# Reordering the routing stage: the shared expert's rows turned and copied earlier, one down product cut in two around the first expert's turned rows

## What is computed

```python
scores = sigmoid(x @ router_w)              # 512 x 64
# the best 4 of 8 groups of experts, in them the best 8 experts of a row
routed = for each expert e: (silu(xb @ w_gate[e]) * (xb @ w_up[e])) @ w_down[e], times the row's weight
shared = (silu(x @ sh_gate) * (x @ sh_up)) @ sh_down      # inner width 256
out = ALPHA * x + routed + shared
```

## Time and profile before

| what | value |
|---|---|
| median of 3 runs | 1092.02 us |
| the profiled execution's own time | 1090.4 us |
| its span, first to last instruction | 1088.6 us |
| PE busy | 1059.9 us, 97% |
| DVE, ACT, POOL busy | 853.4 (78%), 716.7 (66%), 237.1 us (22%) |
| mean granted TensorE clock | 0.997 |
| DMA moved | 294.80 MB, mean 271 GB/s |

### The profile page before, as it was taken

One profiled execution on the slowest core, in us unless ns is written; L12 is line 12 of the kernel. 1 busy time (PEld: TensorE's weight loads), 2 busy tenths in 40 slices (PEclk: granted clock), 3 DMA queues, 4 the chain that ended last, 5 costly groups with the idle time before them and its releaser, 6 DMA issues.

```text
span 1088.6 us, 15813 instructions
## 1 busy us (share of the span) xinstructions
PE 1059.9 (97%) x5382; PEld 864.9 (79%) x5382; DVE 853.4 (78%) x906; ACT 716.7 (66%) x819; POOL 237.1 (22%) x173
## 2 busy tenths in 40 slices
PE   5999999999999999999999999999999999999996
PEld 4778877778888767888888888888888888888585
DVE  6654345663355788999999999999999999999476
ACT  3431244451242527888889988888998888888643
POOL 1000000000005120333333333333333333332101
PEclk9999999999999999999999999999999999999998
DMA  8532221214356449999999999999999999999831
GB/s 296 196 117 78 78 78 39 79 39 155 116 199 237 155 133 347 366 388 391 384 379 384 392 372 392 395 389 388 382 385 374 392 385 390 382 390 342 271 120 61
DMA packets 72571, 294.80 MB, mean 271 GB/s; under 512 B 15312, under 2 KB 18384, under 8 KB 47696
## 3 DMA queue, kind: packets, MB, share of 16 engines
q1 hardware_dynamic: 52944, 256.43, 60.0%
q0 software_dynamic: 19008, 35.71, 12.7%
q10 hardware_dynamic: 576, 2.10, 0.5%
HBM read 283.67 MB, written 44.04 MB: 301 GB/s over the span
## 4 chain that ended last, share of the span: by engine, by line
PE 92%; DMA 3%; DVE 2%; ACT 1%; issue 1%; SPq 0%; DVEq 0%; POOLq 0%; ACTq 0%
PE ps L416 26%; PE ps L418 25%; PE ps L417 25%; PE ps L1562 5%; PE ps L1586 1%; PE ps L1275 1%; PE ps L753 1%; PE ps L777 1%; PE ps L764 1%; DMA residual_rows<-y,put_idx 1%; DMA raw<-in_w_in 1%; DVE w_lo L400 1%; PE ps L325 1%; ACT w_hi L395 1%; PE ps L1546 0%
## 5 line engine op out<-in xcount | busy, mean ns | idle before, releaser
L1825 DVE TENSOR_TENSOR w_lo<-gu_raw,w_hi 128x2048 fp32r<-128x2048 f32 x128 | 292.3, 2284 | 1.0 <-ACT w_hi L1673 1.0
L1673 ACT ACTIVATE w_hi<-gu_raw 128x2048 fp32r<-128x2048 f32 x128 | 245.0, 1916 | 0.0
L416 PE MATMUL ps<-w_hi,xgT_hi 128*128 128x512 f32 x512 | 200.1, 391 | 0.8 <-issue 0.8
L418 PE MATMUL ps<-w_hi,xgT_lo 128*128 128x512 f32 x512 | 199.8, 390 | 0.0
L417 PE MATMUL ps<-w_lo,xgT_hi 128*128 128x512 f32 x512 | 199.2, 389 | 0.0
L1830 DVE TENSOR_TENSOR dn_lo<-dn_raw,dn_hi 128x2048 fp32r<-128x2048 f32 x62 | 142.2, 2293 | 20.8 <-ACT dn_hi L1682 20.8
L416 PE MATMUL ps<-w_hi,act_hi 128*128 128x512 f32 x368 | 146.6, 398 | 0.0
L418 PE MATMUL ps<-w_hi,act_lo 128*128 128x512 f32 x368 | 143.7, 390 | 0.0
L417 PE MATMUL ps<-w_lo,act_hi 128*128 128x512 f32 x368 | 143.4, 390 | 0.0
L1682 ACT ACTIVATE dn_hi<-dn_raw 128x2048 fp32r<-128x2048 f32 x62 | 118.8, 1917 | 0.0
L416 PEld LDWEIGHTS ps<-w_hi,xgT_hi 128*128 128x128 f32 x512 | 96.1, 188 | 21.3 <-issue 1.3
(11 more groups left out here) (218 smaller groups left out, 1763.6 us busy)
## 6 DMA issues: line engine op xcount, KB each, us to landing
gu_raw<-in_moe_w_gate SPq DMA_DIRECT2D x64, 1024.0 KB
gu_raw<-in_moe_w_up SPq DMA_DIRECT2D x64, 1024.0 KB
dn_raw<-in_moe_w_down SPq DMA_DIRECT2D x62, 1024.0 KB
raw<-in_w_in SPq DMA_DIRECT2D x18, 1024.0 KB, 5.2
h_rows<-x_rows SPq DMA_DIRECT2D x8, 512.0 KB, 4.5
raw<-in_w_out SPq DMA_DIRECT2D x4, 1024.0 KB, 4.9
ple_raw<-in_ple_w_gate SPq DMA_DIRECT2D x4, 1024.0 KB, 9.9
x_rows<-in_x SPq DMA_DIRECT2D x4, 512.0 KB, 10.0
```

The lines of the kernel that those rows point to most:

```text
L416: nc.tensor.matmul(out, x_hi, w_hi, start=first, stop=False)
L418: return nc.tensor.matmul(out, x_lo, w_hi, start=False, stop=last)
L1673: nc.scalar.activation(m.w_hi[:, 2 * x.b + half], m.gu_raw[:, 2 * x.b + half], ACT.Copy).then_inc(gu_hi, 1)
L1825: nc.vector.tensor_tensor(m.w_lo[:, 2 * x.b + half], m.gu_raw[:, 2 * x.b + half], m.w_hi[:, 2 * x.b + half].bitcast(F32), ALU.subtract).th ...
```

## The change

On PE, `turn_h(0)` and `turn_h(1)` move up, between the halves of `gate_up(3)`; `turn_h(2)` goes ahead of `down(0)` and `turn_h(3)` behind it; `down(1)` is cut into its two halves, with `turn_x(0)` and the weights' locating between them; the wait for all four copies ahead of `turn_x(0)` becomes one for three, with the fourth ahead of `rounds`; `locate(3)` moves out of the routing into step 0, between the halves of `gate_up(0)`. On ACT, the copies of the turned tiles 0 and 1 go ahead of `silu(3)`, and that of tile 2 ahead of the high parts of expert 1's weights. On DVE, the work between `weigh` and the second `add_rows` is put in another order. No computation is added or removed.

```diff
-    def down(self, pe, t):
+    def down(self, pe, t, halves=(0, 1)):
...
-        for c in range(2):
+        for c in halves:
...
-        last.then_inc(self.summed, 1)
+        if halves[-1] == 1:
+            last.then_inc(self.summed, 1)
...
                 gate_up(x, 0)
+                if first and at == 0:
+                    locate(x.next(3))
...
         routing.gate_up(pe, 3, 0, 4)
         routing.count(pe)
+        routing.turn_h(pe, 0)
+        routing.turn_h(pe, 1)
         routing.gate_up(pe, 3, 4, KD)
         pe.wait_ge(routing.index_base, 1)
         for q in range(2):
             pe.wait_ge(hot_ready, q + 1)
             locate_part(Expert(0, 0, q), ROW_COLS + 8 * q, 0, rows_located)
-        routing.turn_h(pe, 0)
-        routing.turn_h(pe, 1)
+        routing.turn_h(pe, 2)
         routing.down(pe, 0)
-        routing.turn_h(pe, 2)
         routing.turn_h(pe, 3)
-        pe.wait_ge(routing.hT_ready, NT)
+        routing.down(pe, 1, halves=(0,))
+        pe.wait_ge(routing.hT_ready, NT - 1)
         turn_x(Expert(0, 0, 0))
         pe.wait_ge(routing.weighed, 1)
         for q in range(2):
             locate_part(Expert(0, 0, q), WEIGHT_COLS + 8 * q, 3, located)
-        routing.down(pe, 1)
+        routing.down(pe, 1, halves=(1,))
         locate(Expert(0, 0, 2))
-        locate(Expert(0, 0, 3))
+        pe.wait_ge(routing.hT_ready, NT)
         rounds(pe, body, embedding.tensor)
...
         routing.silu(act, 2)
-        routing.silu(act, 3)
         routing.copy_hT(act, 0)
         routing.copy_hT(act, 1)
+        routing.silu(act, 3)
+        routing.copy_hT(act, 2)
         split(Expert(0, 0, 1), 0)
         split(Expert(0, 0, 1), 1)
-        routing.copy_hT(act, 2)
         routing.copy_hT(act, 3)
...
         routing.weigh(dve)
+        one_hot(Expert(0, 0, 2))
+        find_weights()
+        split_x(Expert(0, 0, 0))
+        one_hot(Expert(0, 0, 3))
+        find(Expert(0, 0, 2))
+        list_rows(Expert(0, 0, 2))
         routing.add_rows(dve, 0)
-        find_weights()
-        one_hot(Expert(0, 0, 2))
-        one_hot(Expert(0, 0, 3))
-        split_x(Expert(0, 0, 0))
-        for q in (2, 3):
-            find(Expert(0, 0, q))
-            list_rows(Expert(0, 0, q))
+        find(Expert(0, 0, 3))
+        list_rows(Expert(0, 0, 3))
         routing.add_rows(dve, 1)
```

## The result

The changed kernel takes 1094.23 us, the median of 18 runs (1090.64 to 1097.80); the kernel before 1091.66 us (1090.05 to 1093.88, 18 runs). The ratio is 1.0022, with a 95% interval of 1.0014 to 1.0030: about 2.4 us slower. The forecast of 1093.0 us (1090.8 to 1095.4) holds the time, but of the 2.4 us it has only 1.0 in its sum. It was counted from 1092.02 us, the median of the first 3 runs of the kernel before; counted from 1091.66 us it would have been 1092.7, so the higher start hides 0.4 us of what the sum lacks.

The account below looks back on a forecast made before the run. TensorE was taken to bound the expert loop. 2.24 us won at the first gate-up, 0.2 lost for `locate(3)` and 3.1 in waiting made about +1.0 on 1092.02: 1093.0 us, range 1090.8 to 1095.4.

Parts of the forecast that it names:

- rival (A): Behind the wait at `locate(4)`: TensorE's clock falls to 1.2 GHz, `down(2)` takes 3.5 us more, 1096.5 us; chance 0.13.
- signs of being wrong: `locate(4)` starting before 408.1, matmuls behind the wait standing twice as far apart, or TensorE waiting somewhere after 430.
- TensorE up to the first gate-up: Routing steps on TensorE before expert 0's gate-up, which starts at 399.46 instead of 401.70: 2.24 us won.
- The load of the count: Load into registers ahead of the first gate-up: taken as hidden while `down(1)` runs; if not, 0.4 us more.
- The give-back: After the first gate-up: later `find(3)` delays expert 4's one-hot matrix; `locate(4)` starts 1.03 us later, after waiting 3.1 us.
- Rival (B): At `locate(4)`: expert 4's one-hot matrix is ready when TensorE comes, 2.0 us faster, 1090.0 us; chance 0.06.
- Rival (C): Whole kernel: the parts cancel or VectorE's slack is larger than it looks, nothing seen, 1092.0 us; chance 0.10.
- the slack of 0.6 us: VectorE before the change: expert 4's one-hot matrix ready at 407.42, about 0.6 us to spare before `locate(4)` at 408.13.
- No wait in the loop: Expert loop after expert 1's gate-up, which comes a microsecond later: TensorE has no wait there.

Follow-up runs that it names:

- Put back: Changed kernel with `locate(3)` ahead of the count's load again, all else as changed: 1091.55 us, ratio 1.0000.
- moved alone: Kernel before with only `locate(3)` moved between the halves of expert 0's gate-up: 1094.88 us, ratio 1.0027.
- all three mended: Changed kernel with `down(2)` ahead of `locate(4)`, `add_rows(1)` ahead of `find(3)`, `split_x(1)` ahead of `one_hot(4)` and `one_hot(5)`: 1090.29 us, ratio 0.9987.
- `add_rows(1)` first: Changed kernel with `add_rows(1)` ahead of `find(3)` on VectorE: 1090.90 us, ratio 0.9991.
- all three mended, again: The same kernel as all three mended, measured once more beside its variant with the last store earlier: 1091.15 us, ratio 1.0001.

## Why the prediction was right, and where it was mis-sized

- **By the time it is right, in part by luck.** 1094.23 us lies in the range, which takes its width from the spread of three runs and was meant to leave out rival (A), the clock's fall, priced at 1096.5 us (its upper end, 1093.4 and 1.9 us more, is 1095.3 and not 1095.4). By the mean clock, what happened in most runs was rival (A), at a lower price. And one of the prediction's own signs of being wrong came true in the profiled execution: behind the wait most matmuls of `down(2)` ran at half speed.
- **TensorE up to the first gate-up.** As forecast: `down(0)` at 390.57 (390.39), `turn_x(0)` 395.95 (395.88), `locate(2)` 398.84 (398.84), gate-up 399.42 (399.46), held by the low part of the turned rows for 0.34 us. The load of the count was hidden.
- **The give-back.** `find(3)` 402.51 (402.56), expert 4's matrix done 408.96 (409.01), `locate(4)` 409.06 (409.16), 0.93 us later than before (1.03), wait 2.82 us (3.1). Put back, the loss is gone; moved alone, it is there in full; that is the cause, shown from both sides.
- **What failed: the chance of rival (A).** The prediction took the clock's fall as 0.13 because TensorE was fully busy up to the wait. It fell in the profiled execution and, by the mean clock, in 11 to 14 of 18. Its price was put at 3.5 us, all of `down(2)` at half speed; it was 1.69, since the clock fell only behind the first matmuls of `down(2)` and came back before the gate-up. So the likeliest case was 1.0 + 1.7 = 2.7 us over before, near the 2.57 us between the medians. The matmuls of the earlier trace rows, from which the price was taken, could give neither the price nor the chance. TensorE was as slow before the wait of 3.3 us that stands ahead of them, in its first eight transposes (1.95 us; 1.04 at full speed), and over these rows the profile gives a granted clock of 1.00, so it doesn't explain them:

```profile
10.04 1.95 PE L325 MATMUL ps<-ident,x_rows 128*128 128x128 f32 x8 [10.04 <-DVE x_rows L312]
15.28 2.08 PE L625 MATMUL ps<-w_hi,act_hi 128*128 128x512 f32 x4 [3.30 <-ACT act_hi L331]
```

  And nothing in the rows bore on busy work shielding what follows. The Trainium skill's rule (TensorE: Matmul & The Clock Gate, Why this matters for your kernels), that longer gaps between bursts of matmuls take TensorE's clock back to half, was the better guide. The trace agrees, with 2.82 us of wait and a granted clock of 0.63 from 410 to 414 us; in one execution a wait of 1.76 us was enough, which is less than the skill's page asks for.
- **Rival (B)**, VectorE doesn't bind, was wrong by its own condition. **Rival (C)** too: the slack of 0.6 us was what it looked like.
- **"No wait in the loop"** held but for 0.33 us at 1004.92, and the two profiled spans differ by 3.8 us and not 2.63. The same transposes of the turned activations (`turn_h`, near the loop's end) stand at these times, first in the kernel before, then in the changed one:

```profile
1004.16 0.39 PE L1586 MATMUL ps<-ident,h_ff 128*128 128x128 f32 x2
```

```profile
1004.92 0.47 PE L416 MATMUL ps<-w_hi,xgT_hi 128*128 128x512 f32 x1 [0.33 <-issue]
...
1007.77 0.39 PE L1587 MATMUL ps<-ident,h_ff 128*128 128x128 f32 x2
```

  That is 3.61 us apart; the last `turn_x` rows ahead of them are 3.00 apart (997.55, 1000.55), and at 931 and 934 us 2.61. In the changed kernel's execution ScalarE waited 1.09 us there for the last expert's weights:

```profile
999.44 1.92 ACT L1677 ACTIVATE w_hi<-gu_raw 128x2048 fp32r<-128x2048 f32 x1 [1.09 <-DMA gu_raw<-in_moe_w_up]
```

  Weights come just in time at the loop's end in one execution and not in another. From step 4 to the loop's last `turn_h` the two profiles of one and the same kernel (all three mended) lose 1.9 and 0.4 us against the kernel before, the one with `add_rows(1)` first 3.4 us; those with the longest waits of ScalarE for weights lose most. The medians don't hold this further microsecond, so it belongs to the spread of single executions. What makes the weights late in one and not in another is open.

## What to carry to other kernels

Moving a small producer past a long consumer on one engine is free only on that engine: ask which in-order queue stands waiting for it and what is behind that in the queue. Price a new wait of TensorE with the clock that may fall behind it (here, behind 2.82 us, 1.7 us more in most runs). Filling such a gap with work thrown away took that part back; not making the gap (the locating put back, or VectorE's order mended) took back all of it. When a start is pulled in, look for the next wait with a deadline of its own, here a store among weight loads; without that the gain depended on the execution.

## What the runs showed of the hardware that was not expected

- The clock fell to the 1.2 GHz level behind waits of TensorE of 2.82 us (twice), 2.75 and 1.76 us, and stood at 1.00 behind waits of 1.10 and 1.69 us, in one profiled execution each. In the profile of all three mended, again, it stood behind one of 1.70 us with another of 0.81 us four microseconds on. So waits of 1.69, 1.70 and 1.76 us went either way here; what decides is not shown. In the changed kernel 4 of 18 runs show by their mean clock that it didn't fall.
- The last of ScalarE's four stores of 512 KB took 3.9 us to land in one profile, 5.9 to 6.4 us in six and 10.1 to 11.1 us in three. Issued at 424.74 us in one kernel it took 10.1, at 424.81 us in another 5.9; the cause is open.
- The load of a value into registers, with the branch behind it, stands between `locate(3)` and the first gate-up where TensorE has just waited: 1.01, 1.10 and, in one kernel, 1.55 us from start to start. In `locate(3)` moved alone, where no wait stands just ahead, it is 0.10 us between the last locating and the gate-up.
